# Moving the first gate-up products of a mixture-of-experts loop ahead of the third find and five shared products

## What is computed

```python
def _swiglu(x, w_gu, w_down):
    g, up = jnp.split(x @ w_gu, 2, axis=-1)
    return (jax.nn.silu(g) * up) @ w_down

def _moe(u, router_w, router_b, exp_w_gu, exp_w_down, shared_w_gu, shared_w_down):
    scores = jax.nn.sigmoid((u @ router_w).astype(jnp.float32))
    _, idx = lax.top_k(scores + router_b.astype(jnp.float32), TOP_K)
    ...
    return routed + _swiglu(u, shared_w_gu, shared_w_down)
```

## Time and profile before

| what | value |
|---|---|
| median of 3 runs | 1233.4 us (1233.11, 1233.40, 1236.43) |
| profiled execution, its own time | 1233.88 us |
| its span (first to last instruction) | 1232.1 us |
| busy share: PE, DVE, ACT, POOL | 97%, 56%, 44%, 18% |
| chain of waits: PE, DVE, DMA, ACT | 90%, 4%, 3%, 2% |
| mean DMA rate over the span | 261 GB/s |
| mean granted PE clock | 0.991 of full |

### The profile page before, as it was taken

How to read it: one execution, slowest core, us unless ns; L and a number is a source line. 1 busy time by engine, 2 the same in 40 slices (tenths; PEclk the granted TensorE clock), 3 DMA queues, 4 the chain that set the end, 5 groups by cost and what they waited for, 6 DMA issues and landing times.

```text
span 1232.1 us, 20837 instructions
## 1 busy us (share of the span) xinstructions
PE 1192.7 (97%) x5729; PEld 703.4 (57%) x5730; DVE 690.8 (56%) x1281; ACT 541.3 (44%) x630; POOL 222.4 (18%) x323
## 2 busy tenths in 40 slices
PE   5899999999999999998999999999999999999996
PEld 5687887777888888884444343443434434344342
DVE  4542347586572676867545454454545546555567
ACT  5572224745422413231435454454544546566521
POOL 1000000000000000003332332333323234343300
PEclk9799999999999999999999999999999999999999
DMA  9633503353495485655798889888888888999796
GB/s 342 209 107 115 187 5 103 103 200 126 153 343 186 141 276 197 222 198 240 291 354 326 319 321 340 309 335 314 308 339 301 329 307 326 382 403 417 279 417 268
DMA packets 88593, 321.56 MB, mean 261 GB/s; under 512 B 13040, under 2 KB 16344, under 8 KB 66152
## 3 DMA queue, kind: packets, MB, share of 16 engines
q1 hardware_dynamic: 69192, 279.69, 61.5%
q0 software_dynamic: 14432, 32.85, 7.0%
q10 hardware_dynamic: 4928, 8.49, 2.0%
HBM read 292.35 MB, written 48.24 MB: 276 GB/s over the span
## 4 chain that ended last, share of the span: by engine, by line
PE 90%; DVE 4%; DMA 3%; ACT 2%; SPq 1%; issue 1%; DVEq 0%; ACTq 0%
PE psum L1713 33%; PE psum L1947 28%; PE psum L1957 14%; PE psum L1936 4%; DMA w_now<-expert_rows 2%; PE psum L1686 2%; PE psum L1815 1%; PE psum L1986 1%; PE psum L1746 1%; DMA ring<-in_ada_w 1%; PE psum L1775 1%; PE psum L1804 1%; PE psum L1871 1%; PE psum L1727 1%; PE psum L1863 1%
## 5 line engine op out<-in xcount | busy, mean ns | idle before, releaser
L1947 PE MATMUL psum<-w_now,xT 128*64 128x512 f32 x1568 | 347.3, 595 | 0.0
L1947 PEld LDWEIGHTS psum<-w_now,xT 128*64 128x64 f32 x1568 | 108.2, 137 | 197.2 <-issue 195.9
L1957 PE MATMUL psum<-w_now,mask 128*64 128x512 f32 x784 | 176.6, 592 | 0.0
L1020 ACT ACTIVATE w_now<-stage 128x2048 f32 x79 | 147.7, 1906 | 37.2 <-issue 33.6
L482 DVE TENSOR_TENSOR w_lo<-ring,w_hi 128x1024 fp32r<-128x1024 f32 x80 | 94.7, 1222 | 86.0 <-ACT w_hi L475 84.0
L747 POOL COPY w_now<-stage 128x1024 f32 x79 | 82.0, 1055 | 335.5 <-PE psum L1957 314.6
L1713 PE MATMUL psum<-uT_hi,w_hi 128*128 128x512 f32 x352 | 139.3, 396 | 1.1 <-DVE w_lo L482 1.1
L1713 PE MATMUL psum<-uT_hi,w_lo 128*128 128x512 f32 x352 | 137.0, 389 | 0.0
L1713 PE MATMUL psum<-uT_lo,w_hi 128*128 128x512 f32 x352 | 136.9, 389 | 0.0
L475 ACT ACTIVATE w_hi<-ring 128x1024 fp32r<-128x1024 f32 x80 | 82.7, 1056 | 122.1 <-PE psum L1713 59.5
L1531 DVE COPY w_now<-stage 128x2048 f32 x79 | 95.5, 1242 | 45.7 <-issue 42.0
(11 more groups left out here) (361 smaller groups left out, 1666.4 us busy)
## 6 DMA issues: line engine op xcount, KB each, us to landing
stage<-in_exp_w_gu SPq DMA_DIRECT2D x106, 1024.0 KB, 8.4
stage<-in_exp_w_down SPq DMA_DIRECT2D x53, 1024.0 KB, 5.9
ring<-in_w_in SPq DMA_DIRECT2D x56, 512.0 KB, 5.5
expert_rows<-zero_fill SPq DMA_DIRECT2D x16, 1024.0 KB, 8.2
ring<-in_ada_w SPq DMA_DIRECT2D x32, 512.0 KB, 5.0
stage<-expert_rows SPq DMA_DIRECT2D x12, 1024.0 KB, 18.8
ring<-in_ada_w SPq DMA_DIRECT2D x4, 1024.0 KB, 13.4
scale_w<-in_ada_w SPq DMA_DIRECT2D x4, 1024.0 KB, 14.7
```

Source lines behind the costliest of these rows:

```text
L1020: act.activation(w_now[:, q, 2:4], staged(turns[q] + STAGES - 1, 2, 2), ACT.Copy).then_inc(gu_moved[1], 1)
L1947: mm = pe.matmul(moe_bank(GU)[at, :], xT[:, s % 2, k, at], gu_part(q, k), start=(k == 0), stop=(k == KT - 1))
L1957: mm = pe.matmul(moe_bank(Y0 + g)[at, :], hT[:, j, at], dn_part(q, j, g), start=(j == 0), stop=(j == 1))
```

## The change

PE: find(2) and one shared product go behind turn_rows(0). Then come two shared products and gate_up(0), which so stands ahead of find(3), the last five shared products and turn_rows(1). DVE: move_first(0) goes ahead of find_rows(2) and pick_rows(3), and shared_up(0) goes behind them; shared_up(1) goes behind gated_up(0). ACT: move_second(0) goes ahead of rows_turned(0) and shared_gate(1), and silu(0) ahead of rows_turned(1). No instruction is added or taken away, but one product's place between two finds is closed up.

```diff
@@ ACT, ahead of its loop @@
             act.nop().then_inc(y_ready, 2)
+            act.wait_ge(tables_ready, 1)
+            move_second(0)
             rows_turned(0, 0)
-            act.wait_ge(tables_ready, 1)
             shared_gate(1)
-            move_second(0)
+            silu(0)
             rows_turned(1, 1)
-            silu(0)
             move_down_second(0)
             move_second(1)
@@ DVE, ahead of its loop @@
             pick_rows(2)
-            shared_up(0)
+            move_first(0)
             find_rows(2, 2)
             pick_rows(3)
-            move_first(0)
+            shared_up(0)
             find_rows(3, 3)
             pick_rows(AHEAD)
+            gated_up(0)
             shared_up(1)
-            gated_up(0)
             move_first(1)
@@ PE, ahead of its loop @@
             shared_products(4)
             find(1)
             shared_products(4)
-            find(2)
-            shared_products(1)
             wait_emptied(pe, "bstart_row")
             turn_rows(0, 0, 16)
+            find(2)
             shared_products(2)
-            find(3)
-            shared_products(4)
-            turn_rows(1, 1, 16)
             pe.wait_ge(tables_ready, 1)
             wait_emptied(pe, ("sgu", 0))
             gate_up(0, 0, pe.value_load(copies_thru[0:1, 0:1], min_val=1, max_val=TABLE))
+            find(3)
+            shared_products(5)
+            turn_rows(1, 1, 16)
             wait_emptied(pe, ("sgu", 1))
             wait_emptied(pe, ("sgu", 2))
             wait_emptied(pe, ("sgu", 3))
```

## The result

The changed kernel takes 1243.72 us (median of 5 runs, 1241.23 to 1246.15), the kernel before 1233.46 in the same series. The ratio is 1.0073, with a 95% interval of 1.0049 to 1.0097. Measured again beside the experiments, with 8 runs against 28 of the kernel before (median 1235.99), it is 1241.48 us and 1.0048 [1.0031, 1.0065]. The medians lie 10.3 and 5.5 us apart; by the two ratios the change costs some 9 and 6 us, where I had forecast 1.7 and a range that ended at 1238.0. The forecast was wrong.

What follows compares the result with a forecast made beforehand. PE was taken to bound the kernel, only the stretch ahead of its loop counting. Loop start at 605.05 in place of 603.39 us, +1.66, other terms nothing, moved the median from 1233.4 to about 1235.1 us; range 1232.7 to 1238.0.

Steps and rivals of the forecast that it cites:

- The frame: PE's loop is a rigid train, 11.86 us per step; only a shift of its first step moves the end.
- Step 1: PE starts with turn_rows(0) in place of find(2), waiting for gather 0 until 588.25 us: no gain, loss 0.1.
- Step 2: PE's work from turn_rows(0) to the loop stays 15.26 us; without a new wait the loop starts at 603.5.
- Step 3: Feeding of gate_up(0) by ACT's and DVE's copies: it starts at about 591.1 us, 0.1 late.
- Step 4: Loop's entrance: reads and branches behind the last bank's wait take 1.5 us; loop starts at 605.05, not 603.39.
- The second gate: At the loop's entrance turn_rows(2) needs rows_turned(1), 1.02 us behind turn_rows(1), done at 604.8 us.
- Step 5: SP's loads 2 and 3 go out 7.2 us later, but slots and margins absorb it: cost nothing.
- rival B: Weights come late after SP's delay, PE waits up to 7.2 us: at most 1242.3 us; chance 0.08.
- rival C: PE's clock falls for one gate-up behind the entrance's hole, adding 7.1 us: 1242.2 us; chance 0.04.
- Rival A: Nothing waits at the loop's entrance, the loop starts at 603.5: 1233.5 us; chance 0.13.
- rival D: A gain beyond the bound of PE's only hole, 1.6 us, reaching 3.7 us; chance 0.03.

Runs made afterwards that it cites:

- x_both: Changed kernel with PE's wait for the fourth shared bank moved into the loop and turn_rows(1) ahead of the five products: 1234.77 us.
- x_waits: Changed kernel with PE's wait for the fourth shared bank moved from ahead of the loop to ahead of down_rows in it: 1238.20 us.
- p_gate: Changed kernel with find(2) and one shared product back ahead of turn_rows(0), as in the kernel before: 1241.04 us.
- b_sp: Kernel before with SP's third load held until gate_up(0) has ended: 1236.59 us against 1236.62.
- x_warm2: Changed kernel with 8 filling products of constants ahead of turn_rows(0) and 14 behind turn_rows(1): 1240.56 us.
- x_reads: Changed kernel with three more register reads behind PE's last wait ahead of the loop: 1246.38 us.
- p_swap: Kernel before with only turn_rows(0) put ahead of find(2) and the product behind it: 1235.69 us against 1235.93.
- x_warm: Changed kernel with 16 filling products of constants ahead of turn_rows(0) and 28 behind turn_rows(1): 1246.67 us.
- x_fill: Changed kernel with two more shared products ahead of turn_rows(0), turn_rows(1) ahead of the last three, bank's wait in the loop: 1234.26 us.

## Why the prediction was wrong

The stretch grew by 7.2 us. The runs divide it so: 0.5 for the exchange and the feeding of gate_up(0) (x_both less before), 1.4 for the turned rows at the entrance (x_waits less x_both), 2.2 for what the reads leave bare beyond that (holes of 3.30 and 1.11), and 3.1 for the clock.

I had put that growth at 1.66 us. The 5.5 us between have two main causes. The entrance was sized at 1.5 us and took 3.45: 2.0 us. The clock was left out of the sum, put at nothing from one hole of 1.40 us: 3.1 us. gate_up(0) could start 0.6 us later than I had it, and the work itself ran 0.2 us shorter than in my sum. The longer entrance alone would give 1235.1 + 1.95 = 1237.05 us, still inside my range; with the clock's 3.1 us the sum is 1240.15 and beyond it. The first series' median, 1243.72, lies higher still. What the stretch does not explain of it is not shown to be the change's: the second series has half that excess, and the two profiled spans differ by 3.6 us ahead of anything that the change touches.

- *The frame held.* A rigid loop that moves with its first step: 11.86 us per step, and 564.9 us from first to last down_rows in both. The whole cost lies ahead of it. (There are 49 steps of 32 gate-up records each, 1568 records in all.)
- *Step 1, the exchange,* was right in kind and nearly in size. PE came to turn_rows(0) 5.4 to 5.7 us into the stretch (5.64 and 5.63 in the changed kernel) where I had 5.3. What it did not say is that this hole can let the clock fall.
- *Step 2* held: without the entrance's wait (x_both), PE takes 15.48 us from turn_rows(0) to the loop (588.57 to 604.05), against 15.26 before.
- *Step 3* was right about DVE: 2.36 us, not 3.69, since POOL's copies came later. ACT's copies began 1.6 us behind the tables, not 0.9, so gate_up(0) could start 8.8 us into the stretch at full clock; I had 8.2. With the fallen clock it was 10.3.
- *Step 4, the entrance, failed in its size.* The place, the wait and what is queued behind it were right, the size was not. I took 1.5 us for the reads and branches and 2.5 as a bound, from DVE's idle time around one read. It measures 3.45 us in the changed kernel, and as much in p_gate. No row of before showed this length on PE, and the bound from another engine was no bound. The second gate, the turned rows, was right: x_waits shows its 1.11 us alone.
- *Step 5 and rival B:* no cost, as b_sp shows.
- *The clock, left out of the sum, is the larger failure; rival C came true* with 0.04 of the chance. I had argued from one hole of 1.40 us that the clock is safe, and put the new hole at 1.5. The holes were 1.86 and 3.30, and each was followed by slow records in both traces. The first of them is the wait of step 1, where I looked for no clock cost at all. The price of one gate-up at half the clock, 7.1 us, was too high: it was low for a part of a gate-up only, at some 1.5 us a time. In x_warm2, with the holes filled, the granted clock is 1.00 in both windows shown. The Trainium skill, "TensorE: Matmul & The Clock Gate", section "What's actually happening", says that the throttled state is the default and activity releases it; that run agrees.
- *Rival A* came true only with the waits moved (x_both), and rival D not at all. The hole that I read as 1.6 us ahead of find(2) is 1.40 in its row.

## What to carry to other kernels

Before a wait is put ahead of a loop, look at what is queued behind it on that engine: register reads and branches that cost nothing under long matrix products cost 3.45 us bare, 0.65 for each read that x_reads added. Put the wait at the first use of the bank instead, and let the last work before the loop be something that waits for nobody. Count a hole on PE with what the clock may lose behind it, here some 1.5 us each behind holes of 1.8 and 3.3 us, where it fell, and 2.8 behind one of 5.25, and bound a cost that no row shows by a run, not by another engine's row.

## What I had not expected

- The clock does not follow the hole's length alone. It stayed up behind holes of 1.59, 1.62, 1.76 and 1.93 us (x_waits, p_swap, x_reads, x_both), fell behind 1.84 and 1.86 (the changed kernel, twice), and fell in all four traces with a hole of 3.29 us or more. What tells 1.86 from 1.93 stays open.
- In x_warm2 the last shared bank was empty at 604.15 us, and the filling products ran until 607.43; in x_warm 609.42 and 615.83. Yet a hole of 1.19 us remained, behind 14 products as behind 28. If the entrance takes 3.45 us there too, it began 2.26 us before the last of them ended, in both, which is some 19 records: an estimate. So PE's reads run ahead of its products, but only by so much. Behind a gate-up, five shared products (x_both) or even three (x_fill) no hole is left; a record of a shared product is some four times as long as one of the filling. By how many instructions the reads can run ahead was not tried.
- Filling both holes with useless products took 2.1 us off the stretch of a kernel that is bound by PE (one trace against two).
